# One core, hybrid attention, SSD and expert layer: the product of the SSD branch's y with its output matrix as three rounded products

## The reference

```
proj = h @ w_in                 # q | k | v | z | xBC | dt | gate logits
ya = window_attention(q, k, v) @ w_out_attn
ys = ssd(xBC, z, dt) @ w_out_ssd            # y: (512, 1024), w_out_ssd: (1024, 1024)
gates = sigmoid(g_logit + b_gate)
mix = (gates[0] * ya + gates[1] * ys) @ w_out
h1 = layernorm(alpha * h + mix)
h = layernorm(alpha * h1 + hier_moe(h1) + sigmoid(h1 @ w_ple_gate + b) * (p @ w_ple))
```

## Time and profile before

| | us |
|---|---|
| Median of 3 runs | 848.09 (846.92 to 849.23) |
| The profiled execution's own time | 849.05 |
| Its span, from the first to the last instruction | 847.3 |
| TensorE, VectorE, ScalarE, GpSimd busy | 796.1, 431.7, 176.2, 160.6 |
| Mean granted TensorE clock | 0.981 |

### The profile page before, as it was taken

How to read it: one execution, slowest core, us unless ns; L and a number is a source line. 1 busy time by engine, 2 the same in 40 slices (tenths; PEclk the granted TensorE clock), 3 DMA queues, 4 the chain that set the end, 5 groups by cost and what they waited for, 6 DMA issues and landing times.

```text
span 847.3 us, 10153 instructions
## 1 busy us (share of the span) xinstructions
PE 796.1 (94%) x4045; PEld 534.1 (63%) x4045; DVE 431.7 (51%) x765; ACT 176.2 (21%) x327; POOL 160.6 (19%) x101
## 2 busy tenths in 40 slices
PE   5999999999999999999999999999999999998753
PEld 2987789998878787444444788884545454554221
DVE  6698765767688885112147579262313222301217
ACT  4213325553322230000000200221112111111012
POOL 4924760000323221000000344000000000000052
PEclk9999999999999999999999989999999999999886
DMA  9796331111311224613100631906999999999693
GB/s 302 294 368 143 100 98 52 51 51 51 98 51 51 50 51 142 255 50 100 50 0 1 261 137 51 347 1 268 420 422 421 421 420 424 419 422 423 286 178 120
DMA packets 58920, 166.25 MB, mean 196 GB/s; under 512 B 15813, under 2 KB 38495, under 8 KB 45050
## 3 DMA queue, kind: packets, MB, share of 16 engines
q1 hardware_dynamic: 51748, 139.69, 43.6%
q0 software_dynamic: 6432, 23.77, 8.8%
q10 hardware_dynamic: 694, 2.14, 0.6%
HBM read 147.12 MB, written 22.56 MB: 200 GB/s over the span
## 4 chain that ended last, share of the span: by engine, by line
PE 79%; DMA 11%; DVE 7%; issue 1%; ACT 1%; POOL 1%; SPq 0%; DVEq 0%; POOLq 0%
PE psum L806 24%; PE psum L1119 11%; PE psum L1034 7%; PE psum L1024 6%; PE psum L1073 5%; DMA ring<-in_w_exp_up_dram 5%; PE psum L1134 5%; PE psum L1015 3%; PE psum L1096 3%; PE psum L1097 3%; DMA ring<-in_w_in_dram 3%; DMA arena<-y_rows,rowsU 2%; PE psum L964 2%; PE psum L984 1%; PE psum L1075 1%; PE psum L914 1%
## 5 line engine op out<-in xcount | busy, mean ns | idle before, releaser
L806 PE MATMUL psum<-ring_r 128*128 128x512 f32 (+1 forms) x832 | 214.1, 345 | 4.6 <-DVE arena_r L1533 1.7
L806 PEld LDWEIGHTS psum<-ring_r 128*128 128x128 f32 x832 | 145.1, 191 | 25.7 <-issue 4.4
L1234 ACT COPY arena<-psum 128x256 f32<-128x256 f32 (+4 forms) x104 | 58.4, 579 | 288.2 <-PE psum L1041 139.8
L1119 PE MATMUL psum<-ring,arena 128*64 128x512 f32 x512 | 112.8, 593 | 4.0 <-DMA ring<-in_w_exp_up_dram 3.2
L701 POOL TENSOR_TENSOR ring_r<-ring,ring_r 128x2048 fp32r<-128x2048 f32 x16 | 73.9, 4622 | 204.8 <-ACT ring_r L1234 204.8
L806 PE MATMUL psum<-arena_r,ring_r 128*128 128x512 f32 (+1 forms) x288 | 106.0, 368 | 0.0
L1119 PEld LDWEIGHTS psum<-ring,arena 128*64 128x64 f32 x512 | 38.1, 137 | 76.0 <-issue 75.0
L1981 DVE SCALAR_TENSOR_TENSOR arena<-arena,psum 128x256 f32<-128x256 f32 x16 | 10.0, 624 | 111.3 <-ACT arena L1413 111.3
L1096 PE MATMUL psum<-arena_r 128*128 128x256 f32 x256 | 65.3, 293 | 0.0
L1134 PE MATMUL psum<-ring,arena 128*64 128x512 f32 x256 | 62.2, 631 | 1.6 <-issue 1.6
L754 POOL DMA_INDIRECT y_rows<-arena,storeU x15 | 14.6, 975 | 258.7 <-DVE arena L2012 258.7
(11 more groups left out here) (265 smaller groups left out, 1004.6 us busy)
## 6 DMA issues: line engine op xcount, KB each, us to landing
ring<-in_w_exp_gate_dram SPq DMA_DIRECT2D x32, 1024.0 KB, 11.6
ring<-in_w_exp_up_dram SPq DMA_DIRECT2D x32, 1024.0 KB, 15.6
ring<-in_w_exp_down_dram SPq DMA_DIRECT2D x32, 1024.0 KB, 16.2
ring<-in_w_in_dram SPq DMA_DIRECT2D x18, 1024.0 KB, 5.3
y_rows<-arena POOLq DMA_DIRECT2D x12, 1024.0 KB, 16.9
ring<-in_w_out_ssd_dram SPq DMA_DIRECT2D x4, 1024.0 KB, 7.2
ring<-in_w_out_dram SPq DMA_DIRECT2D x4, 1024.0 KB, 18.5
arena<-in_w_ple_gate_dram SPq DMA_DIRECT2D x4, 1024.0 KB, 7.9
```

Source lines behind the costliest of these rows:

```text
L806: t = mm(o, a, b, start=(first and j == 0), stop=(last and j == 2))
L1119: t = mm(psum[sides[half], parity, :], xgT[buf][:, k, c:c + CAP], ring[:, s:s + 2, k, :], start=(k == 0), stop=(k == KD - 1))
L1234: return nc.scalar.copy(dst, src)
```

## The change

The product `ys` is done with `thrice`: the second output matrix and yT are split in high and low parts.

- Places: the high parts of slices 0 and 1 go to ring slots 6 and 7, of slices 2 and 3 to R_T (`t_r`); low parts are written over the slices in slots 2 to 5. `yT_hi` lies in R_A, where xtok, xdt, xdec and y were; `yT_lo` is written over yT.
- ScalarE, after the last gate: four roundings of a slice as it arrives, then four of the tiles of yT.
- VectorE: the rests of slices 0 and 1 before the first `ya` gate, then, between the gates of `ya` 0 to 3, the rests of yT 0 to 3 and of slices 2 and 3.
- TensorE awaits the four rests of yT before the product, and in it the slice's rest before each k.
- Slices 0 and 1 of `w_out` have slots 0 and 1 in place of 6 and 7, and are loaded after `ya`; slices 2 and 3 keep slots 8 and 9.
- On GpSimd's queue p comes first, and the three row vectors after the end of `ys`.
- Two semaphores are merged with others (w_ple's landing, the zeroing).

```diff
-SLOT_OF = [seq % 4 for seq in range(PROJ)] + [*range(10)]
+SLOT_OF = [seq % 4 for seq in range(PROJ)] + [0, 1, 2, 3, 4, 5, 0, 1, 8, 9]
-FREED = USED[:PROJ - 4] + [USED[q] for q in (16, 17, 18, 19, 18, 19, 19, 19)] + [("ys_read", 2), ("ys_read", 4)]
-MOE_FREED = ([("pe_ya", KD)] * 2 + [("pe_ys", KD)] * 4 + [("pe_mix", 2 * NT)] * 4 + [("ys_read", KD)] * 2)
+FREED = USED[:PROJ - 4] + [USED[q] for q in (16, 17, 18, 19, 18, 19)] + [("pe_ya", KD)] * 2 + [("ys_read", 2), ("ys_read", 4)]
+MOE_FREED = ([("pe_mix", 2 * NT)] * 2 + [("pe_ys", KD)] * 6 + [("pe_mix", 2 * NT)] * 2 + [("ys_read", KD)] * 2)
...
+        yT_hi = shaped(R_A, "p (i k t) -> p i k t", True, i=NT, k=KD, t=P)
+        yT_lo = shaped(R_Z, "p (i k t) -> p i k t", True, i=NT, k=KD, t=P)
+        wos_hi = [shaped(R_RING + s * SLOT, "p (k n) -> p k n", True, k=2, n=D) for s in (6, 7)]
+        wos_hi += [t_r[:, s * SLOT:(s + 1) * SLOT].rearrange("p (k n) -> p k n", k=2) for s in (0, 1)]
+        wos_lo = [shaped(R_RING + s * SLOT, "p (k n) -> p k n", True, k=2, n=D) for s in range(2, 6)]
...
             pool.wait_ge(s_pe_yT, NT)
+            pool.dma_start(p_in, p_v).then_inc(s_p_in, 16)
+            pool.wait_ge(s_pe_ys, KD)
             for dst, name, landed in ((A1w, "ln1_w", s_ln_in), (A1b, "ln1_b", s_ln_in), (bple, "b_ple_gate", s_bple_in)):
                 pool.dma_start(dst, aps[name].broadcast_to([P, D])).then_inc(landed, 16)
-            pool.dma_start(p_in, p_v).then_inc(s_p_in, 16)
...
-            pe.wait_ge(s_yT_read, NT)
-            for s in range(4):
-                arrived(pe, SEQ_WOS + s)
+            pe.wait_ge(s_yT_lo, NT)
             for n in range(KD):
                 o = opened(("ys", n)).rearrange("p (i t) -> p i t", i=NT)
                 for k in range(KD):
-                    s = SLOT_OF[SEQ_WOS + k // 2]
-                    t = mm(o, ringN[:, s, k % 2, n * P:(n + 1) * P], yT[:, :, k, :], start=(k == 0), stop=(k == KD - 1))
+                    s, c = k // 2, slice(n * P, (n + 1) * P)
+                    pe.wait_ge(s_w_lo, PROJ + s + 1)
+                    t = thrice(o, wos_hi[s][:, k % 2, c], wos_lo[s][:, k % 2, c], yT_hi[:, :, k, :], yT_lo[:, :, k, :],
+                               k == 0, k == KD - 1)
                 t.then_inc(s_pe_ys, 1)
...
+            act.wait_ge(s_pe_g, 2 * KD)
+            for s in range(4):
+                arrived(act, SEQ_WOS + s)
+                copy(wos_hi[s], ringN[:, SLOT_OF[SEQ_WOS + s]]).then_inc(s_w_hi, 1)
+            act.wait_ge(s_pe_yT, NT)
+            for c in range(NT):
+                act.wait_ge(s_yT_read, c + 1)
+                copy(yT_hi[:, c], yT[:, c]).then_inc(s_yT_hi, 1)
...
+            def wos_rest(s):
+
+                dve.wait_ge(s_w_lo, PROJ + s)
+                dve.wait_ge(s_w_hi, PROJ + s + 1)
+                v.tensor_tensor(wos_lo[s], ringN[:, SLOT_OF[SEQ_WOS + s]], wos_hi[s].bitcast(F32), ALU.subtract)\
+                    .then_inc(s_w_lo, 1)
+
             dve.wait_ge(s_g_read, 2 * KD)
             dve.wait_ge(s_pe_yT, NT)
+            wos_rest(0)
+            wos_rest(1)
             for n in range(KD):
                 dve.wait_ge(s_pe_ya, n + 1)
                 v.scalar_tensor_tensor(mixT[:, n, :], gact[:, n, 0, :], 1.0, bank(("ya", n)), ALU.add, ALU.mult)\
                     .then_inc(s_ya_read, 1)
+                if n < NT:
+                    dve.wait_ge(s_yT_hi, n + 1)
+                    v.tensor_tensor(yT_lo[:, n], yT[:, n], yT_hi[:, n].bitcast(F32), ALU.subtract).then_inc(s_yT_lo, 1)
+                if n < 2:
+                    wos_rest(2 + n)
```

More of the change, by code:

```diff
@@ L244, in sem @@
             return ctx.enter_context(nc.semaphore(name))
-        with nc.sbuf_tensor("ring_r", [P, RING], F32R) as ring_r, nc.sbuf_tensor("arena_r", [P, ARENA], F32R) as arena_r:
-            pass
+        with nc.sbuf_tensor("ring_r", [P, RING], F32R) as ring_r:
+            with nc.sbuf_tensor("t_r", [P, 4096], F32R) as t_r:
+                pass
+            with nc.sbuf_tensor("arena_r", [P, ARENA], F32R) as arena_r:
+                pass
         ring_words = ctx.enter_context(nc.sbuf_tensor("ring", [P, RING], F32))
@@ L504, in block_kernel @@
         s_hT_hi = sem("hT_hi")
-        s_wple_in = sem("wple_in")
         s_wsmall_in = sem("wsmall_in")
@@ L512, in block_kernel @@
         s_yT_read = sem("yT_read")
+        s_yT_hi = sem("yT_hi")
+        s_yT_lo = sem("yT_lo")
         s_y_act = sem("y_act")
@@ L521, in block_kernel @@
         s_z_read = sem("z_read")
-        s_zero_set = sem("zero_set")
         s_zeroed = sem("zeroed")
@@ L630, in _ @@
             sp.wait_ge(s_pe_mix, 2 * NT)
-            sp.dma_start(wple, aps["w_ple"][0].rearrange("(k p) n -> p k n", p=P)).then_inc(s_wple_in, 16)
+            sp.dma_start(wple, aps["w_ple"][0].rearrange("(k p) n -> p k n", p=P)).then_inc(s_wsmall_in, 16)
             experts(0)
@@ L687, in _ @@
             pool.wait_ge(s_dist_in, 1)
-            g.memset(zt, 0.0).then_inc(s_zero_set, 1)
-            pool.wait_ge(s_zero_set, 1)
+            link(g.memset(zt, 0.0))
             def last_normed(x, w, b, norms):
@@ L1063, in _ @@
             route(logits, NT - 1).then_inc(s_pe_rt, 1)
-            pe.wait_ge(s_wple_in, 16)
+            pe.wait_ge(s_wsmall_in, 16 * 4)
             pe.wait_ge(s_pT_read, 2)
```

## The result

| | before | after |
|---|---|---|
| Median, us | 848.64 (4 runs, 846.92 to 849.23) | 833.22 (4 runs, 832.94 to 837.67) |
| Ratio, 95% interval | | 0.984 (0.982 to 0.987) |
| Profiled execution: span | 847.3 | 831.2 |
| Start of `ys`, start of mix, in that span | 360.53, 417.03 | 360.27, 405.36 |
| All executions of the study: mean (number) | 847.6 (49) | 834.6 (16) |

The first timing says 15.4 us less, the profiled executions 16.1, the means of all executions 12.9. The forecast was 11.2, to 837.0: the median of the first timing, 833.2, lies 0.8 us under the stated range (834.0 to 841.5), the mean of all sixteen executions inside it. The stage gave 11.4; the rest of this document is mostly about the difference.

What follows compares the result with a forecast made beforehand. TensorE, busy 94% of the span and holding 79% of the chain, was taken as the bound. The product gave -11.2 us, preparation, moved loads and waits 0: 848.09 - 11.2 = 836.9, given as 837.0, range 834.0 to 841.5.

Steps and rivals of the forecast that it cites:

- The product, -11.2 us: In `ys`, 192 rounded matmuls at 0.228 us, 43.8 us, replace 64 full float32 ones taking 54.95 us.
- Both bounds kept open for the moving tile's runs and for the 64 waits: In `ys`: 0.228 to 0.429 us per matmul for four short runs; 0 to 1.5 us for the added waits.
- Rival 4 (slower): In `ys`, short moving runs hold rounded matmuls back: gain gone at 0.286 us each, 875 at 0.429; chance 0.04.
- rival 3: In `ys`, a rounded product costs half a float32 piece, 0.215 us: stage 41.2 us, total 834.4; chance 0.04.
- The preparation under `ya`: Under `ya`, 12 us of new VectorE and ScalarE work costs 0; `yT_lo` whole at 358.0, margin 2.5 us.
- T = 343: Before `ys`, last landing of the second output matrix's slices; 342 to 348.6 possible, no cost under 345.5.
- Rival 2: Before `ys`, `yT_lo` is late: 3.1 us stall at T = 348.6, total 840.0, or 843 with halved clock; chance 0.08.
- The moved loads: Later `w_out` slices and row vectors cost 0; the first mix addition might be 3 us late, unseen by TensorE.
- What is next late: After `ys`, everything including the expert stream is tied to TensorE, so the gain passes through to the end.
- rival 5: After `ys`, the gain is given back because expert stream or routing ends at the same time: 848; chance 0.04.
- The clock's luck: Near 500, before and behind the rank product: half-clock variation, allowed 1.5 us together with the waits.
- the distance from mix to the end: From mix's start to span end, 430.3 us; a change over 1.5 us would make the prediction wrong.

Runs made afterwards that it cites:

- Experiment 4: Changed kernel with five extra ScalarE copies of yT's first tile before its rounding, so the yT rests end later: 840.9 us, ratio 0.993.
- experiment 2: Changed kernel with all splits and moved loads kept, but `ys` as one plain float32 product of the high parts: 846.6 us, ratio 0.9989.
- experiment 3: Kernel before with 13 of the 64 `ys` matmuls left out, run twice: mean 836.7 us (ratio 0.986), then 835.7 us (0.985).
- experiment 5: Changed kernel with only the high x high product in `ys`, one rounded product instead of three: 806.1 us, ratio 0.951.
- `one_product`: Changed kernel with one rounded product (high x high) in place of three in `ys`, roundings and waits kept: 806.1 us, ratio 0.951.
- `late_rests`: Changed kernel with five more ScalarE copies ahead of the first yT rounding, delaying the yT rests: 840.9 us, ratio 0.993.

## Why the prediction was right, and where it was off

**The product, -11.2 us: right.** 192 pieces took 43.55 us, forecast 43.8; the gain of the stage was 11.40. Both bounds kept open for the moving tile's runs and for the 64 waits ended at their low end. Rival 4 (slower) is out with that, and so is rival 3: a piece at half of a plain one's 0.429 us would have given 41.2 us.

**The preparation under `ya`: right that it is hidden, with less slack.** I had the last slice at T = 343 and it came at 344.9. The sum of bytes at the full rate was nearly right: from 335 to 343 the DMA engines moved 373 to 422 GB/s, and then almost nothing. But ScalarE could begin only 1.9 us after 343, when the last few packets were in, and for these I had no term. (I also put the rival traffic that leaves at two thirds; by my own list it is 3.5 of 4 MB.) The rest of the chain was shorter than I took it (slice rests 2.28 and not 2.45 us, and operations follow each other with hardly a gap), so the end was 358.5 against 358.0: 1.75 us of slack for 2.5 predicted. Experiment 4 shows that the slack is all there is. Rival 2 was therefore nearer than its 0.08 looked: 1.8 us of later landing would have started it.

**The moved loads: right that they cost nothing** (-0.9, between -2.5 and +0.7, experiment 2). They may even give something: experiments 2 and 3 point the same way, with 0.9 and 1.3 us (1.5 less 0.24 of stage), which would be most of what the stage leaves unexplained. No run shows by which way. The ln1 vectors did become what VectorE waits for, as the text allowed, 0.9 us late and without effect.

**What is next late: right.** Experiments 3 and 5 pass 11.2 and 29.0 us of the stage on to the end; rival 5 is out.

**The clock's luck: mis-sized, and this is the step that failed.** The prediction took the stage's gain from the median of three executions and allowed 1.5 us for waits and clock together, and said that it would be wrong if the distance from mix to the end changed by over 1.5 us. It changed by 4.4. The runs show in its place: 3.4 us less of half clock and a gap of 1.49 us that is not there, and experiment 3 has most of such a difference (430.8 against 427.9) between two profiles of one source. The profiled execution of before was 1.5 us above its kernel's mean over 49 executions (849.05 against 847.6) and that of after 1.7 below (832.94 against 834.6). Together these are 3.2 us of the 16.1. With them taken out the change gives 12.9 us; from the standard deviations (1.7 over 45 executions, 2.25 over 16) that is known to about 1.2 us, so the 11.4 us of the stage lie just below its lower edge, 11.7. Whether the other 1.5 us belong to the change or are chance stays open (experiment 3 leaves the same 1.5 us). The mean granted clock does not explain them: it is 0.980 for both kernels, over 45 and 16 executions. The forecast of 837.0 was on a base of 848.09; on the mean of 847.6 it would have been 836.4, against a mean of 834.6. That the first timing shows 15.4 us where all executions show 12.9 is luck of few executions.

## What to carry to other kernels

Where TensorE holds the chain and VectorE and ScalarE idle beside it, three rounded products for one full float32 product are worth a fifth of the product's time (43.55 for 54.95 us), as long as all splits are ready in time: schedule them from the landing of the last weight slice, and leave room behind the time at which its bytes would be moved at the full rate (here 343, with the wait for it ending at 344.9). The slack then found (here 1.75 us) is worth knowing: lateness of 3.3 us beyond it cost 3.44 us of wait in the profile and 6.8 us of mean time. A profile is one execution: where one kernel's executions spread over 7 us, compare stages between profiles, and totals only between means of many.

## What the runs showed of the hardware that was not expected

- The rounded piece with a 512-column moving tile takes 0.227 us whether the tile is one run or four runs of 128 words.
- Half-clock time came in portions: the sums by single us are 1.70 to 1.71 or 3.41 to 3.42 us in nearly every place between mix and the last matmul, in all profiles (once 5.12, in `one_product`).
- Time and mean granted clock of an execution go together closely on one and the same kernel (-0.92 over 16), with 4 us between the slower and the faster half.
- Six profiles have a gap of 1.46 to 1.49 us ahead of the rank product, and all six have half clock behind it; the three with seven small matmuls in its place have none. The gap of 3.44 us of `late_rests` had none behind it either. The filling did not lower the median of the old kernel.
- The bytes of three slices and p, loaded at once, were all but moved at 343, and the engine that waited for the last of them began at 344.9.
